# Decode sparse attention inside the input projection: all steps of a tile in one block behind the tile's last product

## The chip, the cores and the metric

The kernel runs on one core of a Trainium2 chip. A core has TensorE (PE in the profile, its weight loads PEld), VectorE (DVE), ScalarE (ACT), GpSimd (POOL) and SyncE (SP), which here only issues transfers. Each engine runs its own list of instructions in order, and they meet through semaphores. Sixteen DMA engines serve the queues of SP, ACT and POOL. The metric is the device time of one launch in microseconds. Differences under 0.5% are what a measurement of this kernel can't tell from none.

## The reference

One inference step of a one-layer decoder with a prompt of 512 rows and 8 sampled sequences of 4 new rows behind 2048 cached positions. Everything is float32.

```python
z = einsum('btd,de->bte', x, w_in) + b_in        # 1024 -> 27 tiles of 128 columns
# mLSTM heads (8): conv of width 4 over q,k; silu; chunkwise recurrence over 64 rows; head norm; sigmoid gate
# sparse attention heads (8 query, 2 key/value), three branches per query, each a masked softmax
s_c = q . k_cmp + bias; o_c = softmax(s_c) . v_cmp      # keys pooled by 32 positions
score = sum of p_c over heads and pairs of pooled blocks # importance of a block of 64
top_i = top_k(score, 16)                                # the current block always in
s_s = q . k[top_i] + bias; o_s = softmax(s_s) . v[top_i]
s_w = q . k_window + bias; o_w = softmax(s_w) . v_window # last 512 positions
mix = concat(mlstm, gate_c*o_c + gate_s*o_s + gate_w*o_w) @ w_out
x1 = LN(ALPHA*x + mix); y = LN(ALPHA*x1 + ffn(x1))      # gated ConvFFN, 2688 wide
```

The keys and values of the 2048 cached positions lie in pages of 128 positions, found through a page table; the last 512 positions have a cache of their own for the window branch.

## The kernel before

Activations are kept transposed, features on the partitions and the 544 rows (512 prompt rows, 32 sampled rows) in the free dimension. A float32 product is made of three fp32r products: ScalarE writes the high part of a weight tile (`split_hi`, L415), VectorE the low part (`split_lo`, L423), two tiles ahead. `project` (L1489) runs the 48 products of one weight tile. SyncE loads weight tiles into a ring of four.

The order of the work is written out by hand, the same on every engine:

1. Input projection, 27 tiles: eight mLSTM q/k tiles (VectorE does the convolution of each, ScalarE the silu), four output-gate tiles, the gate tile `Z_G`, four mLSTM value tiles, four attention query tiles and six attention key/value tiles. Outputs alternate between `q4[0]` and `q4[1]` (banks 0 to 3).
2. Gate transposes and token transposes (L1531, L1555).
3. mLSTM over the prompt (L1559 on) and over the sampled rows (L1634 on).
4. Sparse attention over the prompt (L1690 on). It needs a table of relative biases. It is written to DRAM (`relrow`, L475: the whole of it from 8 partitions) after the last weight load is issued, and read back skewed (`tb`, L479) once it has landed. SyncE waits in between. SyncE also issues there `out_win_s` (4 MB, DRAM to DRAM), `out_zkv`, `out_mconv` and the tiny `out_m_p` (L480 to L486), and waits for them (L488).
5. Sparse attention over the sampled rows, "decode" (L1779 to L1979). Two groups of four sequences. Per group 4 window key bundles (4 transposes each) and 16 quads of pages (`page_keys`: 4 key transposes; `compress`: 8 pooling products). Every fourth quad is followed by a score set (`scores_d`). Bundles of transposes rotate over three banks (`T_BANKS`), and ScalarE copies each to SBUF (`keys_t`, L771). Pages come through a ring of 8 slots in 192 KB transfers (SyncE the even ones, GpSimd the odd ones). Selected values have a place of their own for all 64 pages of a group. Softmaxes, selection (`select`, L1357: a rank by 32 x 32 comparisons in five passes over 1024 elements) and outputs of group g-1 lie between the quads of group g; those of the last group come at the end.
6. Output projection, first norm, 42 up tiles, 24 down parts, second norm.

Where a wait is for a page:

```python
pe.wait_ge(pg_land[o % PAGE_RING], 16 * (o // PAGE_RING + 1))
mm = pe.transpose(t[:, 128 * k:128 * k + 128], pages[:, o % PAGE_RING, 256:384], ident)
```

Of the kernel before, what the change touches and what calls it, by code (L numbers as in the profile page):

```python
# [24 lines left out]
T = 512  # L25
# [18 lines left out]
KEY_BUNDLES = SG + SG * QUADS  # L44
SETS = 1 + QUADS
KEY_RING = 6
T_BANKS = 3
BUNDLES = 1 + KEY_BUNDLES + 2 + 2
LATE = 6
# [14 lines left out]
Z_MQ, Z_MK, Z_MO, Z_G, Z_MV, Z_NQ = 0, 4, 8, 12, 13, 17  # L64
Z_CK, Z_CV, Z_SK, Z_SV, Z_WK, Z_WV = 21, 22, 23, 24, 25, 26
# [3 lines left out]
def table(*widths):  # L69

    at, n = {}, 0
    for name, w in widths:
# [8 lines left out]
                      ("maskw", 512), ("maskn", 64), ("tie", 1024), ("jsum", 128), ("headmask", 8), ("kvmask", 2))  # L81
# [12 lines left out]
def constants():  # L94
# [18 lines left out]
    c["tie"] = np.broadcast_to((r[None, :] < r[:, None]).reshape(1, 1024), (128, 1024))  # L113
# [24 lines left out]
    return a128, a32, rel.astype(f)  # L138


def layer(nc, a):
    with ExitStack() as ctx:
# [26 lines left out]
        tvs = wring[0:32, 3, 0:512]  # L169
        gf = sb("gf", [8, NT])  # L170
# [13 lines left out]
        wpad = sb("wpad", [128, NG * (4 + 80 + CW)])  # L184
# [24 lines left out]
        wslide = wpad[:, 168:].rearrange("p (e c) -> p e c", e=2)  # L209
# [7 lines left out]
        uq = smem[:, 0:1142].rearrange("p (s c) -> p s c", s=2)  # L217
        tq = smem[:, 1142:2284].rearrange("p (s c) -> p s c", s=2)
        hm = smem[:, 2284:2476].rearrange("p (n c) -> p n c", n=8)
        mc = smem[:, 2476:2692].rearrange("p (n c) -> p n c", n=8)  # L220
# [9 lines left out]
        hc = zt[:, 13:17, :].rearrange("p k c -> p (k c)")[:, 0:2048].rearrange("p (j h d) -> p j h d", j=4, h=H)  # L230
# [6 lines left out]
        def by_block(ap):  # L237
# [7 lines left out]
        gd = work[0:32, 3072:3328]  # L245

# [8 lines left out]
        wvs = zt[0:32, 0, 0:512]  # L255
        wks = zt[0:32, 1, 0:512]
# [27 lines left out]
        flat = zt[:, :, :].rearrange("p k c -> p (k c)")  # L284
        pages = wring[:, :, :].rearrange("p s c -> p (s c)")[:, 0:PAGE_RING * 384] \
            .rearrange("p (s c) -> p s c", s=PAGE_RING)

        vsel = [t[:, 0:SG * PAGES * 128].rearrange("p (s k c) -> p s k c", s=SG, k=PAGES) for t in (flat, arena)]
        wk = [w.rearrange("p (k c) -> p k c", k=4) for w in (arena[:, 8192:8704], arena[:, 8704:9216],
                                                            flat[:, 11424:11936], flat[:, 11936:12448])]  # L290
        wvl = arena[:, 9216:11264].rearrange("p (s k c) -> p s k c", s=SG, k=4)
        score = smem[:, :].rearrange("p (g c) -> p g c", g=GROUPS)
        pts = whi_f[:, :, :].rearrange("p s c -> p (s c)")
        biasw = work[:, 0:512]
        biasn = work[:, 512:576].rearrange("p (g c) -> p g c", g=GROUPS)
        biasc = work[:, 576:640]
        skt = [work[:, 640:1152], work[:, 1152:1664], wring[:, 3, 0:512], wring[:, 3, 512:1024],
               zt[:, Z_SV, 0:512], zt[:, Z_WV, 0:512]]
        sw = work[:, 1664:2208]
        pc = work[:, 2208:2272]  # L300
        kct = zt[:, Z_WK, 0:256].rearrange("p (s n) -> p s n", s=SG)
        vcs = work[:, 2400:3424].rearrange("p (b c) -> p b c", b=NB)
        ptw = work[:, 3424:3936]
        ptc = work[:, 3936:4064]
        craw = zt[:, Z_SK, 0:512].rearrange("p (s c) -> p s c", s=SG)
        qb = work[:, 4064:4320].rearrange("p (b m) -> p b m", b=NB)
        rk1 = flat[:, 8704:9728].rearrange("p (j i) -> p j i", j=NBLK)
        rk2 = flat[:, 9728:10752].rearrange("p (j i) -> p j i", j=NBLK)
        gtmp, osb = flat[:, 8704:8752], flat[:, 8704:8832]
        pext = flat[:, 9728:9856]  # L310
        impt, rank, pair = (flat[:, 10752 + 32 * k:10784 + 32 * k] for k in range(3))
        ptn = flat[0:32, 10880:11136].rearrange("p (k c) -> p k c", k=2)
        vnt = flat[0:32, 11136:11392].rearrange("p (k c) -> p k c", k=2)
        st = sm[:, 0:16]
        gr = sm[:, 16:24]
# [53 lines left out]
        v_land = [sem(f"v_land{i}") for i in range(3)]  # L369
        wk_land = sem("wk_land")  # L370
# [7 lines left out]
        nd_ow, nd_o, nd_oc, nd_ot, nd_mx = (sem(n) for n in ("nd_ow", "nd_o", "nd_oc", "nd_ot", "nd_mx"))  # L378
# [51 lines left out]
        def pool_rows(eng, n):  # L430

            page = eng.value_load(ptab[0:1, n:n + 1], min_val=0, max_val=POOL_PAGES - 1)
            return a["pool"][bass.DynSlice(page, 1), :, :].rearrange("a p c -> (a p) c")

        def page_at(o):

            g, u, s, k = o // (SG * PAGES), o // (4 * SG) % QUADS, o // 4 % SG, o % 4
            return (SG * g + s) * PAGES + 4 * u + k

        def page_values(eng, n, rows, landed):  # L440
            g, m = n // (SG * PAGES), n % (SG * PAGES)
            eng.dma_start(vsel[g][:, m // PAGES, m % PAGES, :], rows[:, 384:512]).then_inc(landed, 16)

        def page_keys(eng, o, rows):
            eng.dma_start(pages[:, o % PAGE_RING, :], rows[:, 0:384]).then_inc(pg_land[o % PAGE_RING], 16)

        def stream_page(eng, o, part):

            n = page_at(o)
            if o >= PAGE_RING:  # L450
                rows = pool_rows(eng, n)
                eng.wait_ge(pg_used, o - PAGE_RING + 1)
                page_keys(eng, o, rows)
                if n >= SG * PAGES:
                    page_values(eng, n, rows, v_land[1 + part])
# [4 lines left out]
        def _(sp):  # L460
# [10 lines left out]
            for i in range(2, I_OUT):  # L471
                load_weights(i)
            sp.wait_ge(rel_sb, 1)

            sp.dma_start(relrow.ap(), ohp[0:8, NREL:2 * NREL].unsqueeze(1).broadcast_to([8, 128, NREL])).then_inc(rel_out, 16)  # L475
            sp.wait_ge(rel_out, 16)

            shifted = bass.AP(tensor=relrow, offset=127, ap=[[NREL - 1, 128], [128 * NREL, H], [1, 512]])
            sp.dma_start(tb, shifted).then_inc(tb_in, 16)  # L479
            sp.dma_start(a["out_win_s"], a["win"][:, TS:, :]).then_inc(stored, 16)  # L480
            sp.wait_ge(z_dve, ZT - Z_MV)
            sp.dma_start(a["out_zkv"], zt[:, Z_CK:ZT, :]).then_inc(stored, 16)
            sp.wait_ge(conv_done, Z_MO)
            sp.dma_start(a["out_mconv"], mc).then_inc(stored, 16)
            sp.wait_ge(g_rdy, 1)
            sp.dma_start(a["out_m_p"], lnb[:, T - 1:T]).then_inc(stored, 16)  # L486

            sp.wait_ge(stored, 48 + 16)  # L488
            sp.wait_ge(silu_done, Z_MO)
# [3 lines left out]
            sp.dma_start(n0, a["n0"]).then_inc(sd_in, 16)  # L493
            sp.wait_ge(ml_ce, QT)
# [10 lines left out]

            for n in range(SG * PAGES):
                rows = pool_rows(sp, n)
                page_values(sp, n, rows, v_land[0])
            for o in range(0, PAGE_RING, 2):
                page_keys(sp, o, pool_rows(sp, page_at(o)))  # L510
            sp.wait_ge(np_mx, QT)
            sp.wait_ge(nd_pp, 1)

            def window(b):
                return a["win"][b].rearrange("(k p) c -> p k c", k=4)

            def window_keys(b):
                sp.dma_start(wk[b % SG], window(b)[:, :, 0:128]).then_inc(wk_land, 16)

            def window_values(b):  # L520
                sp.dma_start(wvl[:, b % SG], window(b)[:, :, 128:256]).then_inc(wv_land, 16)

            for s in range(SG):
                window_keys(s)
            for g in range(GROUPS):
                if g >= 1:
                    sp.wait_ge(nd_ow, g)
                for s in range(SG):
                    window_values(SG * g + s)
                for o in range(SG * PAGES * g, SG * PAGES * (g + 1), 2):  # L530
                    stream_page(sp, o, 0)
                    if o == SG * PAGES * g + 4 * SG and g + 1 < GROUPS:

                        sp.wait_ge(nd_s, SETS * g + 1)
                        for s in range(SG):
                            window_keys(SG * (g + 1) + s)
            sp.wait_ge(pg_used, NB * PAGES)
            sp.wait_ge(nd_s, SETS * GROUPS)
            for i in range(I_OUT, I_OUT + RING):
                load_weights(i)  # L540

            sp.wait_ge(nd_mx, GROUPS)
            for k in range(KD):
                sp.dma_start(xt[:, k, :], a["xt"][:, k, :]).then_inc(xin2, 16)
            sp.dma_start(hf, a["hf"]).then_inc(hist, 16)
# [12 lines left out]
        def _(pool):  # L558
# [49 lines left out]
            for o in range(1, PAGE_RING, 2):  # L608
                page_keys(pool, o, pool_rows(pool, page_at(o)))
# [1536 lines left out]
```

## Time and profile before

| | us |
|---|---|
| median of 3 runs | 1099.0 (1095.66 to 1100.27) |
| profiled execution | 1103.59 |
| its span, first to last instruction | 1101.9 |
| TensorE busy | 943.0 (86%) |
| VectorE / ScalarE / GpSimd busy | 535.0 / 359.1 / 78.4 |
| mean granted TensorE clock | 0.859 |

The span divides, by TensorE's instructions, into input projection (12 to 189), token transposes and mLSTM (189 to 306), prompt attention (306 to 424), decode attention (424 to 600), output projection and first norm (600 to 688), up and down projection and second norm (688 to 1102). A granted clock of 1.00 is 2.4 GHz, 0.50 is 1.2 GHz. A busy TensorE is not one at its peak, since matmul records overlap.

### The profile page before, as it was taken

The page shows a single profiled execution, that of the slowest core. Times are in us where ns is not written, and L with a number is a line of the kernel's source. Part 1 is how long each engine was busy: PE and PEld are TensorE (multiplying, and loading weights), DVE is VectorE, ACT ScalarE, POOL GpSimd, SP SyncE. Part 2 cuts the span into 40 slices and gives each one's busy share as a digit, 9 for nine tenths or more (in the row PEclk, how much of TensorE's full clock was granted, in tenths as well). Part 3 has the DMA queues.
Part 4 walks back from the last instruction along what each step waited for, and adds up shares of the span by engine and source line. Part 5 has one row for each costly group of instructions (what it writes and reads, how often), then busy time and mean ns, then how long its engine had stood idle before and what let it go on. Part 6 is the DMA issues. An engine that isn't in the chain of part 4 may idle for free.

```text
span 1101.9 us, 18710 instructions
## 1 busy us (share of the span) xinstructions
PE 943.0 (86%) x7389; PEld 827.2 (75%) x7389; DVE 535.0 (49%) x1095; ACT 359.1 (33%) x729; POOL 78.4 (7%) x124
## 2 busy tenths in 40 slices
PE   4999999875789886677764995999999999999993
PEld 4999999564465554344433984999999999999992
DVE  4653423556546672102526326667666676522225
ACT  3444111211034563113224115443434344322214
POOL 2000100200200000234420000000000000000000
PEclk9999899755556998666576996999999999999997
DMA  7222224361032202778762320222222222222212
GB/s 254 77 97 81 73 79 66 48 274 64 5 115 60 73 1 78 239 210 261 243 215 65 107 77 0 77 87 87 96 78 97 77 96 76 89 85 78 82 48 81
DMA packets 58376, 112.82 MB, mean 102 GB/s; under 512 B 6817, under 2 KB 36290, under 8 KB 57714
## 3 DMA queue, kind: packets, MB, share of 16 engines
q1 hardware_dynamic: 52304, 94.83, 27.2%
q0 software_dynamic: 5120, 14.69, 4.3%
q10 hardware_dynamic: 866, 2.13, 0.5%
q8 instruction: 58, 0.95, 0.3%
q14 instruction: 28, 0.23, 0.1%
HBM read 103.40 MB, written 12.38 MB: 105 GB/s over the span
## 4 chain that ended last, share of the span: by engine, by line
PE 74%; DVE 9%; DMA 7%; ACT 4%; issue 4%; SPq 1%; POOLq 0%; POOL 0%; ACTq 0%; DVEq 0%
PE q L1505 28%; PE q L1503 25%; DMA wring<-in_pool 5%; PE q L1718 2%; PE q L1847 2%; PE q L1746 2%; PE q L1736 2%; PE q L1983 1%; PE q L1606 1%; PE q L1984 1%; DMA xt<-in_xt 1%; PE q L1820 1%; PE q L1660 1%; ACT whi L740 1%; PE q L1708 1%
## 5 line engine op out<-in xcount | busy, mean ns | idle before, releaser
L413 DVE TENSOR_TENSOR wring_r<-wring,whi_r 128x1024 fp32r<-128x1024 f32 (+1 forms) x101 | 121.2, 1201 | 289.6 <-ACT whi_r L410 289.5
L410 ACT ACTIVATE whi_r<-wring 128x1024 fp32r<-128x1024 f32 (+1 forms) x101 | 104.3, 1033 | 390.7 <-PE q L1505 387.3
L1505 PE MATMUL q<-xt_r,whi_r 128*128 128x288 f32 x552 | 165.3, 299 | 0.0
L1503 PE MATMUL q<-xt_r,whi_r 128*128 128x256 f32 x552 | 156.1, 283 | 0.0
L1503 PE MATMUL q<-arena_r,whi_r 128*128 128x256 f32 x440 | 128.2, 291 | 21.6 <-DVE xt_r L413 13.7
L1505 PE MATMUL q<-arena_r,whi_r 128*128 128x288 f32 x440 | 132.1, 300 | 0.0
L1505 PE MATMUL q<-arena_r,wring_r 128*128 128x288 f32 x440 | 131.8, 300 | 0.0
L1503 PE MATMUL q<-arena_r,wring_r 128*128 128x256 f32 x440 | 124.7, 283 | 0.0
L1503 PE MATMUL q<-mixt_r,whi_r 128*128 128x256 f32 x400 | 113.1, 283 | 10.5 <-DVE xt_r L413 10.5
L1505 PE MATMUL q<-mixt_r,whi_r 128*128 128x288 f32 x400 | 119.4, 298 | 0.0
L1503 PEld LDWEIGHTS q<-xt_r,whi_r 128*128 128x128 f32 x552 | 105.4, 191 | 0.0
L1505 PEld LDWEIGHTS q<-xt_r,whi_r 128*128 128x128 f32 x552 | 105.2, 191 | 0.0
L1503 PEld LDWEIGHTS q<-arena_r,whi_r 128*128 128x128 f32 x440 | 84.4, 192 | 23.7 <-DVE wring_r L413 12.7
L1505 PE MATMUL q<-mixt_r,wring_r 128*128 128x288 f32 x336 | 100.1, 298 | 0.0
L1503 PE MATMUL q<-mixt_r,wring_r 128*128 128x256 f32 x336 | 94.4, 281 | 0.0
L1505 PEld LDWEIGHTS q<-arena_r,whi_r 128*128 128x128 f32 x440 | 84.3, 192 | 0.6
L1503 PEld LDWEIGHTS q<-mixt_r,whi_r 128*128 128x128 f32 x400 | 76.1, 190 | 11.1 <-issue 10.9
L1503 PEld LDWEIGHTS q<-arena_r,wring_r 128*128 128x128 f32 x440 | 84.2, 191 | 0.0
L1505 PEld LDWEIGHTS q<-arena_r,wring_r 128*128 128x128 f32 x440 | 84.1, 191 | 0.0
L1505 PEld LDWEIGHTS q<-mixt_r,whi_r 128*128 128x128 f32 x400 | 76.0, 190 | 0.0
L1820 PE MATMUL q<-cst,wring 128*128 128x128 f32 x128 | 40.2, 390 | 27.7 <-DMA wring<-in_pool 27.0
L1503 PEld LDWEIGHTS q<-mixt_r,wring_r 128*128 128x128 f32 x336 | 63.5, 189 | 0.0
(395 smaller groups left out, 1656.3 us busy)
## 6 DMA issues: line engine op xcount, KB each, us to landing
wring<-in_w_up SPq DMA_DIRECT2D x42, 512.0 KB, 3.2
wring<-in_w_in SPq DMA_DIRECT2D x27, 512.0 KB, 3.3
wring<-in_pool POOLq DMA_DIRECT2D x64, 192.0 KB, 3.6
wring<-in_pool SPq DMA_DIRECT2D x64, 192.0 KB, 3.5
wring<-in_w_down SPq DMA_DIRECT2D x24, 448.0 KB, 3.2
zt<-in_pool SPq DMA_DIRECT2D x64, 64.0 KB, 1.9
wring<-in_w_out SPq DMA_DIRECT2D x8, 512.0 KB, 4.2
out_win_s<-in_win SPq DMA_DIRECT2D x1, 4064.0 KB
```

The costliest lines, as they stand in the source:

```text
L410: return eng.activation(out, src, ACT.Copy)
L413: return eng.tensor_tensor(out, src, hi.bitcast(F32), ALU.subtract)
L740: act.activation(ptb[:, m % 2, g, 0:w], bank[4 + g][:, 0:w], ACT.Copy).then_inc(np_te, 1)
L1503: pe.matmul(out[:, 0, 0:HALF], w, x[:, 0:HALF], start=(kk == 0 and n == 0), stop=(end and n == 2))
L1505: mm = pe.matmul(out[:, 1, 0:HALF + NS], w, x[:, HALF:NT], start=(kk == 0 and n == 0), stop=(end and n == 2))
L1606: mm = pe.matmul(bank[4 + q][:, 65 * t:65 * t + 65], whi_f[:, c % 2, 512 * q + 128 * t:512 * q + 128 * t + 128], tv[:, c, 2 * t + q, :], s ...
L1660: mm = pe.matmul(bank[2 + c][0:32, HD * t:HD * t + HD], qm[half(c), t].rearrange("p b x -> p (b x)")[:, 32 * b:32 * b + 32], ctv[half(c), ...
L1718: return pe.matmul(bank[6][p, 128 * j:128 * j + 128], v, probs, start=start, stop=stop, skip_group_check=True)
L1736: mm = pe.matmul(bank[2 * (m % 2) + g][:, 0:w], q_of(GQ * g + j, i), zt[64 * g:64 * g + 64, (Z_SK, Z_WK)[k], 0:w], start=True, stop=True)
L1746: mm = pe.transpose(bank[4 + g][:, 128 * kk:128 * kk + 128], pb[:, m % 3, g, 128 * kk:128 * kk + 128], ident)
L1820: mm = pe.transpose(t[:, 128 * k:128 * k + 128], pages[:, o % PAGE_RING, 256:384], ident)
L1847: mm = pe.matmul(bank[2 + s // 2][32 * k:32 * k + 32, at + 128 * e:at + 128 * e + 128], wslide[:, e, 12 - 4 * u:44 - 4 * u], pg, start=(u ...
```

## The change

The decode attention is no stage of its own. The columns of `w_in` are reordered: gate tile first, then queries (1 to 4), sampled keys and values (5 to 10), the mLSTM q/k tiles (11 to 18), output gates (19 to 22), mLSTM values (23 to 26). The decode work is cut into beats (g, i), i = -4..-1 a window key bundle, i = 0..15 a quad of pages, each of two halves: h = 0 the key transposes, pooling and score set, h = 1 everything else of that beat (softmax steps and outputs, mostly of group g-1). All engines walk the same list of halves. Five halves go to each of tiles 5 to 20, four to each of tiles 21 to 25 and three to tile 26. All halves of a tile run behind its last product.

```diff
+def halves_of_tiles():
+    body = [x for x in decode_halves() if x[0] < GROUPS]
+    tail = [x for x in decode_halves() if x[0] >= GROUPS]
+    out = [[] for _ in range(ZT)]
+    for n, x in enumerate(body):
+        t = len(body) // (TAIL - FIRST)          # FIRST, TAIL = 5, 21
+        out[FIRST + n // t].append((KD - 1, x))
+    for n, x in enumerate(tail):
+        out[TAIL + n // 4].append((KD - 1, x))
 ...
             def project(out, first, parts, hi, lo, kt, split=None, between=()):
 ...
+                        if k == kt - 1:
+                            mm.then_inc(w_used, 1)
+                        for at, half in between:
+                            if at == k:
+                                decode_half(*half)
```

All transposes go through one bank (`bank[5]`), and each bundle waits for the copy of the one before:

```diff
+            def bundle(*name):
+                if BUNDLE[name] >= 1:
+                    pe.wait_ge(nd_te, BUNDLE[name])
+                return bank[5]
 ...
+                    for h in range(NG):
+                        for k in range(4):
+                            pg = pages[:, ring_item(g, i, k) % PAGE_RING, 128 * e + 64 * h:128 * e + 64 * h + 64]
+                            mm = pe.matmul(bank[4][32 * k:32 * k + 32, 128 * s + 64 * e:128 * s + 64 * e + 64],
+                                           wslide[:, e, h, 12 - 4 * u:44 - 4 * u], pg, ...
```

The pooling is thus 16 calls of 64 columns in one bank. The score sets use bank 6 and four key buffers alone. The page ring keeps its 8 slots; window keys go through it too (two slots a bundle), and values through a ring of four slots of 4 x 64 KB. ScalarE and VectorE run a tile's halves ahead of that tile's split and eviction:

```diff
+            for n in range(ZT):
+                for _, half in HALVES[n]:
+                    decode_half(*half)
+                if n + 2 < ZT:
+                    split_hi(act, n + 2)
```

SyncE's list is now (GpSimd's has the other half of the pages and no weights):

```diff
+            for i in range(2, RING):
                 load_weights(i)
+            for n in range(ZT):
+                if n == 4:
+                    sp.wait_ge(rel_sb, 1)
+                    sp.wait_ge(consts, NCONST)
+                    sp.dma_start(relrow.ap(), ohp[0:8, NREL:2 * NREL].unsqueeze(1).broadcast_to([8, 128, NREL])) \
+                        .then_inc(rel_out, 16)
+                    for i in range(-SG, 0):
+                        stream_keys(sp, mybir.EngineType.SP, 0, 0, i)
+                        issued[0] += 1
+                for _, (g, i, h) in HALVES[n]:
+                    stream(sp, mybir.EngineType.SP, 0, issued, g, i, h)
+                if n + RING < I_OUT:
+                    load_weights(n + RING)
```

`stream` asks for the keys of the beats up to two ahead, each slot when it is free, and for a chunk of values when its slot is. The selection is rewritten (`max`, `match_replace` twice, on 32 values) in place of the 32 x 32 comparisons. `tb` is read back behind the whole decode work (`nd_mx`). `out_win_s` and `hf` are issued before the prompt attention ends, the first four output weights at the end of the input projection. The gate exponentials run at tile 4. The results of the decode attention wait in `mixd` and are copied to `mixt` ahead of the prompt attention.

## Rows read from the trace of the kernel before

**Rows 1.** Stages: us, busy us of each engine (instructions), granted clock, DMA share, GB/s
```profile
112.00:191.00 79.00, 78.31 (x609) 77.93 (x609) 26.98 (x49) 10.95 (x11) 4.38 (x3) 0.96 0.29 70
203.00:262.00 59.00, 40.56 (x227) 32.62 (x228) 34.43 (x59) 6.14 (x7) 5.78 (x4) 0.51 0.52 171
424.00:600.00 176.00, 117.56 (x1212) 68.25 (x1212) 46.06 (x95) 44.41 (x98) 49.77 (x93) 0.67 0.63 195
```
**Rows 2.** Timeline, ScalarE's splits released by a tile's end: start, us, what, wait
```profile
60.45 1.06 ACT L410 ACTIVATE whi_r<-wring 128x1024 fp32r<-128x1024 f32 x1 [3.48 <-PE q L1505]
66.49 1.06 ACT L410 ACTIVATE whi_r<-wring 128x1024 fp32r<-128x1024 f32 x1 [3.48 <-PE q L1505]
```
**Rows 3.** Waits, 424 to 600 us: us in total, times, longest
```profile
PE q L1820 <- DMA wring<-in_pool: 27.0, 35, 3.5
```
**Rows 4.** Timeline, first and last instruction of the decode attention
```profile
424.79 1.13 PE L1779 MATMUL q<-cst,relp 128*128 128x512 f32 x2 [0.79 <-DVE mixt L1267]
...
599.12 0.46 DVE L1385 COPY mixt<-q 64x64 f32<-64x64 f32 x2 [0.42 <-PE q L1870]
```
**Rows 5.** Timeline, prices of the decode steps at either clock
```profile
440.43 0.66 PE L1820 MATMUL q<-cst,wring 128*128 128x128 f32 x4
441.01 0.64 PE L1847 MATMUL q<-wring,wpad 128*32 128x128 f32 x16
441.12 0.60 ACT L776 ACTIVATE zt<-q 128x512 f32<-128x512 f32 x1 [2.12 <-PE q L1820]
...
505.12 1.08 PE L1847 MATMUL q<-wring,wpad 128*32 128x128 f32 x16
505.98 1.07 PE L1834 MATMUL q<-wring,xt 128*32 128x512 f32 x2
506.84 1.07 PE L1834 MATMUL q<-zt,xt 128*32 128x512 f32 x2
...
594.09 1.08 PE L1883 MATMUL q<-arena,whi 128*32 128x128 f32 x32
```
**Rows 6.** Page issues: an issue, us to landing by kind, rate of group 1's stretch
```profile
441.24 0.54 POOL L445 DMA_DIRECT2D wring<-in_pool  x1 [0.63 <-issue]
wring<-in_pool POOLq DMA_DIRECT2D x64, 192.0 KB, 3.6
505.00:567.00 62.00, 48.28 (x555) 28.20 (x558) 18.59 (x30) 15.80 (x29) 30.15 (x56) 0.67 0.77 239
```
**Rows 7.** VectorE and ScalarE by form, 424 to 600 us: busy, mean ns, idle before
```profile
L1369 DVE TENSOR_TENSOR smem<-smem,zt 128x2048 f32<-128x2048 f32 x2 | 4.6, 2292 | 0.1
L1316 DVE TENSOR_REDUCE sm<-smem 128x1 f32<-128x2080 f32 x2 | 4.6, 2320 | 0.1
L818 ACT ACTIVATE smem<-smem,sm 128x2080 f32<-128x2080 f32 x2 | 4.1, 2029 | 13.6 <-DVE sm L1317 13.6
```
**Rows 8.** The bias table's transfer: issue, SyncE's wait for it, DMA meanwhile
```profile
164.43 0.88 SPq L475 DMA_DIRECT2D relrow<-smem  x1
SPq L479 <- DMA relrow<-smem: 54.1, 1, 54.1
170.00:180.00 10.00, 10.00 (x82) 10.00 (x81) 4.09 (x6) 2.12 (x2) 0.00 (x0) 1.00 0.43 51
```
**Rows 9.** Small transfers behind large ones of their queue
```profile
5.44 0.34 ACTq L629 DMA_DIRECT2D sm<-in_m  x1
18.21 2.51 POOL L569 COPY mixt<-cst 8x1024 f32<-8x1024 f32 x2 [13.94 <-DMA sm<-in_m]
SPq L490 <- DMA out_m_p<-lnb: 29.2, 1, 29.2
```
**Rows 10.** The clock behind a wait, and in part-busy stretches
```profile
108.00:112.00 4.00, 0.66 (x6) 0.45 (x4) 3.89 (x7) 1.06 (x1) 1.29 (x1) 1.00 0.38 131
112.00:119.00 7.00, 6.31 (x28) 6.31 (x29) 3.36 (x5) 0.00 (x0) 4.22 (x2) 0.51 0.01 2
552.00:557.00 5.00, 3.50 (x65) 2.19 (x63) 0.75 (x1) 1.20 (x2) 3.21 (x6) 1.00 0.94 295
```

More of the change, by code:

```diff
@@ L299, in layer @@
[L299 to L308, printed above, removed]
@@ L444, in page_keys, with page_rows @@
[L444 to L455, printed above, removed]
+        def page_rows(eng, first, step, n):
+            _, ids = nc.values_load_multi_w_load_instructions(ptab[0:1, first:first + step * (n - 1) + 1:step], engines=(eng,),
+                                                              min_val=0, max_val=POOL_PAGES - 1)
+            return [a["pool"][bass.DynSlice(page, 1), :, :].rearrange("a p c -> (a p) c") for page in ids]
@@ L504, in _ @@
             sp.wait_ge(sd_end, 2)
[L506 to L510, printed above, removed]
-            sp.wait_ge(np_mx, QT)
[L512 to L542, printed above, removed]
+            sp.wait_ge(st_cs, 16)
+            sp.wait_ge(stored, 64)
+            sp.dma_start(a["out_win_s"], a["win"][:, TS:, :]).then_inc(stored, 16)
+            sp.dma_start(hf, a["hf"]).then_inc(hist, 16)
+            sp.wait_ge(np_mx, QT)
             for k in range(KD):
                 sp.dma_start(xt[:, k, :], a["xt"][:, k, :]).then_inc(xin2, 16)
-            sp.dma_start(hf, a["hf"]).then_inc(hist, 16)
             for i in range(I_OUT + RING, len(ITEMS)):
@@ L1488, in _, with project @@
         def _(pe):
-            def project(out, first, parts, hi, lo, kt, split=None):
+            def project(out, first, parts, hi, lo, kt, split=None, between=()):
                 for c in range(parts):
@@ new lines, in copied, with on_chip, window_keys @@
+            def copied(*name):
+                pe.wait_ge(nd_te, BUNDLE[name] + 1)
+            def on_chip(g, i, k):
+                o = ring_item(g, i, k)
+                pe.wait_ge(pg_land[o % PAGE_RING], 16 * (o // PAGE_RING + 1))
+                return pages[:, o % PAGE_RING, :]
+            def window_keys(g, i):
+                t = bundle("keys", g, i)
+                for w in range(2):
+                    chunk = on_chip(g, i, w)
+                    for k in range(2):
+                        mm = pe.transpose(t[:, 256 * w + 128 * k:256 * w + 128 * k + 128], chunk[:, 128 * k:128 * k + 128],
+                                          ident)
+                mm.then_inc(nd_t, 1)
@@ new lines, in scores_d @@
+            def scores_d(g, j):
+                n = SETS * g + j
+                copied("keys", g, SG * j - 1)
+                if n >= 1:
+                    before, was = (n - 1) // SETS, (n - 1) % SETS
+                    if was == 0:
+                        pe.wait_ge(nd_wr, before + 1)
+                    else:
+                        pe.wait_ge(nd_se, QUADS * before + was)
+                for s in range(SG):
+                    mm = pe.matmul(bank[6][ROWS * s:ROWS * s + ROWS, :], qb[:, SG * g + s, :], skt[s], start=True, stop=True)
+                mm.then_inc(nd_s, 1)
@@ new lines, in window_t, with output @@
+            def window_t(g, new):
+                pe.wait_ge(nw_p, g + 1)
+                t = bundle("window", g, new)
+                if new:
+                    mm = pe.transpose(t[0:32, 0:128], sw[:, 512:544], ident)
+                else:
+                    for k in range(4):
+                        mm = pe.transpose(t[:, 128 * k:128 * k + 128], sw[:, 128 * k:128 * k + 128], ident)
+                mm.then_inc(nd_t, 1)
+            def output(s, probs, v, start=False, stop=False):
+                return pe.matmul(bank[7][ROWS * s:ROWS * s + ROWS, 0:128], probs[:, ROWS * s:ROWS * s + ROWS], v,
+                                 start=start, stop=stop, skip_group_check=True)
@@ new lines, in outputs_window @@
+            def outputs_window(p):
+                copied("window", p, True)
+                copied("new_values")
+                pe.wait_ge(wv_land, 16 * SG * (p + 1))
+                if p >= 1:
+                    pe.wait_ge(nd_mx, p)
+                for s in range(SG):
+                    output(s, ptn[:, 1, :], vnt[:, 1, :], start=True)
+                for k in range(4):
+                    for s in range(SG):
+                        mm = output(s, ptw[:, 128 * k:128 * k + 128], vring[:, k, s, :])
+                    mm.then_inc(v_used, 1)
@@ new lines, in importance_t, with outputs_compressed @@
+            def importance_t(p):
+                pe.wait_ge(nc_pr, p + 1)
+                t = bundle("importance", p)
+                pe.matmul(t[:, 0:32], k128("jsum"), pair, start=True, stop=True)
+                pe.wait_ge(nc_p, NG * (p + 1))
+                pe.transpose(t[:, 128:256], pext, ident).then_inc(nd_t, 1)
+            def outputs_compressed(p):
+                copied("importance", p)
+                for s in range(SG):
+                    output(s, ptc, vcs[:, s, :].unsqueeze(1).broadcast_to([128, NG, HD]))
@@ new lines, in selected_t @@
+            def selected_t(p, k):
+                pe.wait_ge(ns_p, 5 * p + k + 1)
+                t = bundle("selected", p, k)
+                if k < 4:
+                    for c in range(4):
+                        mm = pe.transpose(t[:, 128 * c:128 * c + 128], score[:, p, 512 * k + 128 * c:512 * k + 128 * c + 128],
+                                          ident)
+                else:
+                    mm = pe.transpose(t[0:32, 0:128], score[:, p, PAST:SCW], ident)
+                mm.then_inc(nd_t, 1)
```

1174 lines of the change are left out of this document (618 added, 556 removed).

## The prediction

> **What bounds the kernel now.** I read the table of stages first, then the waits of the stage that moves, then single instructions for prices. The input projection is dense: TensorE is busy 79 of 79 us at nearly full clock, a tile every 6.04 us [rows 1, 2]. The decode attention is the opposite: 176 us in which TensorE is busy 118 at a mean clock of 0.67 while DMA moves 195 GB/s [rows 1]. Its largest wait on TensorE is for pages, 27.0 us [rows 3]. From its first product at 424.79 to its last copy at 599.58 [rows 4] nothing of the other stages runs: 174.8 us on the path, and all of it goes. The question is what the same work costs behind 22 of the 27 tiles (5 to 26), since TensorE does it between two tiles and not beside them.
>
> **The change part by part.** Sums are for the profiled execution, 1103.6 us with a span of 1101.9; the median of the three timed runs, 1099.0, is 4.6 lower, and I subtract the same 4.6 at the end.
>
> *TensorE's own decode work.* At full clock four key transposes take 0.58 us (440.43 to 441.01), a quad's pooling (8 calls, 16 records) about 0.57, 16 output calls 1.08 (32 records at 594.09) [rows 5]. Per group of four sequences: 20 key bundles x 0.58 = 11.6; 16 poolings. These become 16 calls of 64 columns instead of 8 of 128: not below 0.57 (same columns), not above 1.08 (what the old form takes at half clock, when each call costs double); I take 0.65, near the low end, because the columns that pass are the same and four calls run beside each other on 32 array columns each: 10.4. Five score sets: four calls of 512 columns are 8 records in two waves 0.85 apart at half clock (505.98, 506.84, the last ending at 507.91) [rows 5]; I take 1.0 at full: 5.0. 92 output calls, 16 in 1.08 with the last one's tail: 5.8. 28 other transposes x 0.145: 4.1. Small products: 1. That is 38, twice 76 us.
>
> *Waits in the blocks.* (a) All bundles now share one bank (bank 5), so each waits for ScalarE's copy of the one before: 0.60 us [rows 5] and two hand-overs, 0.85. Behind a page bundle the pooling covers 0.65: 32 x 0.2 = 6. Behind the eight window bundles nothing does: 6. Behind some 20 others 5. Together 17. (b) Pages. The ring holds 2 beats (8 pages). Five halves a tile are 3 page beats in tiles 7, 9, 11, 15, 17, 19 and 2 in the others. Two beats lie ready when a block begins, since 6 us of projection cover them; the third is asked for when the first is used up. Two issues per queue at 0.54 and 3.6 to landing [rows 6] make 4.7, less one beat (1.43) in between: 3.2 x 6 = 19. SyncE's weight loads queue behind these page requests, but four weights are in the ring, so they are not late. (c) Values: four chunk slots, asked for two beats before use in the same block. With 4 issues x 0.54 and 3.6 to landing, 5.8 less some 1.7 of work: 4 each in tiles 24 and 25, 2 in tile 18: 10. (d) Chains. Tile 23 waits for select and softmax: the bias and the maximum over 2048 scores are 2.29 and 2.32, the exp 2.03 [rows 7], plus the new selection (six small DVE operations, at about 0.2 as the others of 32 to 64 columns) and a table load. That makes 9.8, of which 6.0 are covered by tile 23's products. The old ranking (five passes over 1024 elements) is gone from this chain. Tiles 13 and 21 run scores, ScalarE's compressed copies, transposes and scores again in one block, 2 each. Together 8. Sum of waits 54; blocks 76 + 54 = 130 us, or 5.9 us per tile. VectorE and ScalarE take 46 and 44 us of decode work into a phase that is now about 300 us long; their own loads there, 27 and 11 in 79 us of its second half [rows 1], leave room, and splits are a tile ahead.
>
> *A transfer that is moved.* The bias table's rows (relrow, 2560 KB from 8 partitions) went out at 164.43, after the last weight load; SyncE then stood 54.1 us until they had landed, and nobody noticed, as nothing was due [rows 8]. Meanwhile DMA stood at a share of 0.43 and 51 GB/s: a slow transfer that fills some 7 of 16 engines. In the new order it is issued after tile 3 (about 43 us: 42.3 and 0.9 of set-up), with tile 5's window keys right behind it on the same queue. Is a queue served in order? ScalarE's last constant, 1 KB, was issued at 5.44 and freed GpSimd at 18.21; out_m_p, a few bytes behind the 4 MB of out_win_s, kept SyncE for 29.2 us [rows 9]. So small transfers do wait behind large ones of their queue. Window keys of SyncE's half then land at 43 + 55 + 1 = 99 us. Tile 5 ends at about 59: before, tile 6 ended at 60.4 [rows 2], tile 5 at 54.4; 1.2 come on for the gate transposes that stood behind the last tile and 3.6 for set-up (below). TensorE waits 40 us in the first block, with all queued behind it. From both sides: 0, if rows of one queue overtake each other, or 45, if GpSimd's half of the keys shares those engines. I take 40, the value of the two rows.
>
> *Clock.* One wait of 4.0 us in the old projection (for a tile's eviction, 108 to 112) was followed by 7 us at 0.51, i.e. at 1.2 GHz, then 2.4 GHz again [rows 10]: half of 6.8 us is lost, 3.4. I count the blocks with a wait of 3 us or more: 5, 7, 9, 11, 15, 17, 19, 23, 24, 25, ten x 3.4 = 34. Bounds: 0, if busy ends of a block keep the clock, and 22 x 3.4 = 75.
>
> A rule of the Trainium skill speaks against the change here. "TensorE: Matmul & The Clock Gate", section "HAM oscillation — how this bites in real kernels": short bursts of products separated by waits for DMA start every burst at the half rate. By it each of the 21 later blocks costs its 3.4, a sum 37 us higher than mine; the decode stage of before (0.67) goes with the rule, the wait of 4.0 us shows one such fall.
>
> *Small terms.* Set-up products now ahead of tiles 2 and 5 add 0.9 + 0.6, and tile 5 waits 2.1 for the sample queries (copies of 0.74, 0.24 and small ones): 3.6. The gate tile comes first, so the 4.0 us wait and its clock loss go: -7.4. Exponentials of the gates are ready long before the mLSTM (ScalarE's table load 1.28 after the token transposes stood on its path): -2.5. Output weights and history, read earlier, are hidden before and after. The 4 MB window copy moves under the prompt attention (51 GB/s there, share 0.17 over 118 us, so room): 0; if that cover failed its 29 us would have to be met by the reload of xt.
>
> Sum: 130 + 40 + 34 + 3.6 - 7.4 - 2.5 = 198, against 174.8: +23 us, 1127 in the profiled execution, **1122 us** against the median.
>
> **Rivals.** (1) *The table's rows do not hold up the queue.* Then the 40 us go and its clock fall: 1122 - 43 = 1079, faster. It decides by the moment SyncE's first window keys land: before 76 us (99 - 23) the change gains. For it: nothing in the trace ran behind relrow, and a share of 0.43 leaves over half of the engines free; against it: the two waits of [rows 9]. (2) *Full clock and covered waits.* Blocks end in products, and page beats keep TensorE some 85% busy; clock 0 to 7 instead of 34, which gives 1088 to 1095, faster. For it: 552 to 557 ran at 1.00 with TensorE 70% busy [rows 10]. Against: a wait of 3 us stands in six blocks. (3) *The clock falls at every block*, since even a block without a page wait leaves TensorE idle during each copy: 22 falls of 3.4 instead of 10, 1122 + 41 = 1163. For it: 203 to 262, TensorE busy 41 of 59 us in gaps of 1 to 4 us, had 0.51 [rows 1]. Against: after the one wait of 4.0 the clock was back within 7 us, and blocks of 4 us hold 3 of products. It is the case of the skill's rule above. (4) *DMA becomes the bound* in group 1: 12.6 MB keys, 5.3 values, 1.1 window keys, 4.2 weights, 1.7 output, 24.8 MB, at 239 GB/s [rows 6] 104 us for tiles 13 to 20, where my blocks and products come to 8 x 6.04 + 53 + 10 = 112. So it costs nothing unless the rate falls below 221; at 200 it adds 12.
>
> **How the numbers follow.** Forecast with its mechanism (with or without (4)) 0.54, its own range 1100 to 1145; (1) 0.16; (2) 0.16; (3) 0.14. A measurement of this kernel tells 0.5%, 5.5 us, from no change. Of the forecast's 0.54, 0.06 lies within 0.5% (waits and clock at their low ends); of (1) 0.13 is faster and 0.03 the same; of (2) 0.15 and 0.01. So faster 0.28, same 0.10, slower 0.62. The range reaches from (1) into (3): 1075 to 1168.
>
> **What would show it.** After: TensorE idle from about 59 to 99 us, with SyncE's window keys as releaser (right), or tile 6's products at about 63 (rival 1). Block lengths alternating by 3 us between tiles 7 and 12; a granted clock of 0.5 in the first microseconds of the products behind tiles 7, 9, 11, 1.00 behind 8 and 10 (rival 3: behind all). End of the projection at about 188 + 200 = 388 us; the prompt attention followed within 1 us by the output projection. My forecast is wrong if the blocks cost over 7 or under 5 us a tile beside the first, or if ScalarE's order (a wait for VectorE's maximum ahead of a key copy) stops TensorE for long, which I have put at nothing because each such step falls behind a page wait.

## The result and the profile after

| | before | after |
|---|---|---|
| timed runs, median (range) | 1099.63 us (1095.66 to 1101.08) | 1109.92 us (1106.5 to 1112.78) |
| profiled execution; its span | 1103.59; 1101.9 us | 1106.5; 1104.4 us |
| mean granted clock | 0.859 | 0.879 |

The kernel is slower: the ratio is 1.0112, with an interval of 1.0083 to 1.0141, so 9 to 15.5 us. The two profiled executions lie only 2.9 us apart: the one of after was the fastest of its four, the one of before (1103.59) was slower than all four timed ones. I had subtracted the same 4.6 us on both sides; what follows accounts for the profiled 2.5 us of span, and the other 8 us between the medians can't be read from a trace.

The stages of after, by windows (columns as in [rows 1]): the last products of tile 5, the wait behind them, and everything from there to the last product of the projection.

```profile
53.00:61.50 8.50, 8.47 (x48) 8.35 (x48) 0.00 (x0) 0.00 (x0) 0.00 (x0) 0.70 0.43 49
61.50:101.70 40.20, 3.06 (x13) 2.19 (x13) 0.00 (x0) 1.19 (x2) 1.12 (x2) 0.54 0.49 79
101.70:369.30 267.60, 225.54 (x2716) 192.93 (x2714) 87.90 (x172) 93.73 (x176) 78.35 (x136) 0.91 0.57 179
```

One window holds three key bundles and nothing else for 40 us. Then 21 tiles (6 to 26) with 20 blocks between them (a block is the decode work behind a tile's last product) run with TensorE 84% busy at a clock of 0.91, against 67% and 0.67 in the old decode stage [rows 1]. TensorE's waits between 50 and 370 us (total, times, longest), which answer to [rows 3]:

```profile
PE q L1653 <- DMA arena<-in_win: 35.8, 1, 35.8
PE q L1733 <- DMA arena<-in_pool: 15.3, 8, 3.6
PE q L1661 <- DMA arena<-in_pool: 8.9, 10, 1.5
PE q L1767 <- DVE smem L1188: 5.5, 1, 5.5
```

These are the window keys, the values, the pages and the selected probabilities. SyncE's own timeline shows why the first is long: its four requests for window keys took 37.2 us to issue behind the table's rows, where the same four take 2.9 us elsewhere (below).

```profile
41.50 0.86 SPq L568 DMA_DIRECT2D relrow<-smem  x1
42.40 37.20 SPq L505 DMA_DIRECT2D arena<-in_win  x4
79.64 10.89 SPq L555 DMA_DIRECT2D wring<-in_w_in  x1
```

Now the blocks. Windows over the products of tile 7, the block behind them (three page beats), the products of tile 8 and those of tile 9:

```profile
113.16:119.16 6.00, 6.00 (x54) 6.00 (x48) 2.64 (x4) 1.07 (x2) 1.07 (x2) 1.00 0.65 221
119.28:126.10 6.82, 4.02 (x110) 2.75 (x108) 0.00 (x0) 1.67 (x3) 2.15 (x4) 1.00 0.54 178
126.10:133.62 7.52, 7.52 (x54) 7.52 (x48) 2.04 (x3) 1.07 (x2) 1.08 (x2) 0.77 0.64 226
138.43:144.43 6.00, 6.00 (x53) 6.00 (x48) 3.12 (x7) 1.07 (x2) 1.07 (x2) 1.00 0.86 291
```

A tile is 6.00 us of products at full clock; tile 8 took 7.52 because part of it ran at 1.2 GHz (0.77 in the mean), tile 9 was whole again. Inside the block of tile 7 the third beat waits for its pages (timeline; the bracket is the idle time and what ended it):

```profile
121.16 0.65 PE L1673 MATMUL q<-arena,wpad 128*32 128x64 f32 x32
123.31 0.30 PE L1661 MATMUL q<-cst,arena 128*128 128x128 f32 x1 [1.49 <-DMA arena<-in_pool]
124.46 0.44 PE L1661 MATMUL q<-cst,arena 128*128 128x128 f32 x2 [0.85 <-DMA arena<-in_pool]
125.26 0.33 PE L1661 MATMUL q<-cst,arena 128*128 128x128 f32 x1 [0.36 <-DMA arena<-in_pool]
```

From last product to first product (the last 0.3 us of the last product counted in) the blocks of tiles 6 to 12 took 3.59, 6.94, 4.81, 6.46, 4.00, 8.14 and 2.59 us. The longest are 19 (12.58), 24 and 25 (11.22 and 11.25): values are what they wait for. The projection ends at 369.0 us, and the output projection begins at 604.62.

### The profile page after: what moved, and what is told of

Its sections match the earlier page's. It is cut to its first block, busy times and chain, and to the rows that moved or that the text cites. A ratio compares the mean times of both kernels' runs of the same rounds, so it can differ in the third digit from the quotient of the medians.

```text
span 1104.4 us, 19843 instructions
## 1 busy us (share of the span) xinstructions
PE 925.0 (84%) x7903; PEld 826.8 (75%) x7903; DVE 520.7 (47%) x1100; ACT 373.2 (34%) x742; POOL 99.5 (9%) x164
## 4 chain that ended last, share of the span: by engine, by line
PE 72%; DVE 8%; issue 5%; ACT 5%; another core or an unknown queue 3%; DMA 3%; SPq 3%; POOLq 1%; POOL 0%; ACTq 0%; DVEq 0%
PE q L1624 28%; PE q L1622 25%; DMA arena<-in_pool 3%; PE q L2061 2%; PE q L2079 2%; PE q L2089 2%; PE q L1949 1%; PE q L2003 1%; PE q L2122 1%; PE q L2123 1%; SPq L477 1%; PE q L1661 1%; PE q L1673 1%; DVE xt L1486 1%
## 5 line engine op out<-in xcount | busy, mean ns | idle before, releaser
L1624 PE MATMUL q<-xt_r,whi_r 128*128 128x288 f32 x552 | 168.4, 305 | 0.0
L1622 PE MATMUL q<-xt_r,whi_r 128*128 128x256 f32 x552 | 158.9, 288 | 0.0
L1622 PE MATMUL q<-arena_r,whi_r 128*128 128x256 f32 x440 | 133.4, 303 | 19.9 <-DVE xt_r L458 11.8
L1624 PE MATMUL q<-arena_r,whi_r 128*128 128x288 f32 x440 | 135.1, 307 | 0.0
L1624 PE MATMUL q<-arena_r,wring_r 128*128 128x288 f32 x440 | 134.4, 305 | 0.0
L1622 PE MATMUL q<-arena_r,wring_r 128*128 128x256 f32 x440 | 127.3, 289 | 0.0
L1622 PE MATMUL q<-mixt_r,whi_r 128*128 128x256 f32 x400 | 112.9, 282 | 10.6 <-DVE xt_r L458 10.5
L1622 PEld LDWEIGHTS q<-xt_r,whi_r 128*128 128x128 f32 x552 | 108.5, 197 | 0.0
L1624 PEld LDWEIGHTS q<-xt_r,whi_r 128*128 128x128 f32 x552 | 108.3, 196 | 0.0
L1622 PEld LDWEIGHTS q<-arena_r,whi_r 128*128 128x128 f32 x440 | 87.8, 199 | 22.6 <-DVE wring_r L458 11.7
L1624 PEld LDWEIGHTS q<-arena_r,whi_r 128*128 128x128 f32 x440 | 87.5, 199 | 0.6
L1622 PEld LDWEIGHTS q<-arena_r,wring_r 128*128 128x128 f32 x440 | 87.1, 198 | 0.0
L1624 PEld LDWEIGHTS q<-arena_r,wring_r 128*128 128x128 f32 x440 | 86.9, 197 | 0.0
L744 ACT ACTIVATE mixt<-q 128x512 f32<-128x512 f32 x40 | 23.9, 596 | 144.1 <-PE q L1661 82.6
```

The source lines that it names most:

```text
L744: act.activation(skt[i % SG], t, ACT.Copy).then_inc(nd_te, 1)
L1622: pe.matmul(out[:, 0, 0:HALF], w, x[:, 0:HALF], start=(kk == 0 and n == 0), stop=(end and n == 2))
L1624: mm = pe.matmul(out[:, 1, 0:HALF + NS], w, x[:, HALF:NT], start=(kk == 0 and n == 0), stop=(end and n == 2))
```

## The experiments

Times are ratios to the kernel before, run on the same chip in turn; "against after" is their quotient with 1.0112 times 1099. Edits are against the changed kernel where nothing else is said.

**Table rows on ScalarE's queue.**

```
-  sp.dma_start(relrow.ap(), ohp[0:8, NREL:2 * NREL] ...)      # SyncE, n == 4
+  act.dma_start(relrow.ap(), ohp[0:8, NREL:2 * NREL] ...)     # ScalarE, n == 4
```

> The changed kernel, with one move: the bias table's rows (2560 KB from 8 partitions) go out on ScalarE's DMA queue instead of SyncE's, at the same point (after tile 3). Queue theory (window keys stood behind these rows on one queue): the wait of 35.8 us in the first block goes and that block falls from 40.4 to about 5 us, so the time is 33 to 38 us below the changed kernel's 1109.9, about 1074; SyncE's four window-key issues no longer take 37 us. Rival (the rows keep 8 of the 16 DMA engines busy, and any transfer beside them is slow, whatever its queue): window keys still land after 80 us, the first block keeps over 20 us, and the time stays above 1095.

Measured: 1.0005 (0.9978 to 1.0031), 12 us below after. Neither theory holds alone. The queue is a third of it: SyncE's requests no longer stand 37 us, and the first keys are there sooner. But they come one by one, behind waits of 4.5, 6.0 and 6.0 us. SyncE's issues, then TensorE's waits in the first block (timelines):

```profile
42.06 15.78 SPq L505 DMA_DIRECT2D arena<-in_win  x4
```
```profile
66.48 1.11 PE L1654 MATMUL q<-cst,arena 128*128 128x128 f32 x4 [4.51 <-DMA arena<-in_win]
73.64 1.09 PE L1654 MATMUL q<-cst,arena 128*128 128x128 f32 x4 [6.04 <-DMA arena<-in_win]
80.73 1.09 PE L1654 MATMUL q<-cst,arena 128*128 128x128 f32 x4 [6.01 <-DMA arena<-in_win]
```

The blocks of tiles 5, 6, 7 took 19.8, 10.5 and 8.2 us here (40.4, 3.6, 6.9 in after). In the trace's packets the rows are 1024 packets of 2560 bytes, 0.36 us each in the steady stretch and some 19 a microsecond: seven engines' worth. The keys are packets of 512 bytes, 0.03 us each. In after, half of each key request (128 of 256 packets) passed at 62 to 81 us while the rows went out, and the other halves came together at 94 to 98. That the first halves went by the engines left free and the second by those that the rows filled is my reading: the records name no engine. With a queue of their own the keys' packets pass between the long ones, some 19 a microsecond like these. So the larger part is the share of the engines, and a second queue only lets the small transfers take turns. The Trainium skill says this of two issuing engines ("DMA: Bandwidth & Descriptors", section "Issuing engines are not separate DMA queues": all run on the same 16 engines and interleave); by it the second queue saves only the time to issue. This run agrees in that some 25 us of the 37 stayed. What it saved is 12 us, and SyncE's four issues fell from 37.2 to 15.8.

**Table rows behind the window keys.** The two statements at n == 4 on SyncE are swapped.

> The changed kernel, with one swap on SyncE's queue: the four window-key requests first, the bias table's rows behind them. Theory (the rows hold up whatever is behind them on the queue and what shares their DMA engines): the first block falls to about 5 us, but the next page requests are behind the rows, so the block of tile 6 takes over a wait that ends near 100 us; the time is 0 to 8 us below the changed kernel's 1109.9. Rival (it was only the place ahead of the first keys that hurt): over 25 us gained.

Measured: 1.0042 (1.0017 to 1.0067), 8 us below after: as the theory had it, at the end of its range. The block of tile 5 took 3.17 us, that of tile 6 took 33.5:

```profile
41.12 2.93 SPq L505 DMA_DIRECT2D arena<-in_win  x4
44.10 0.87 SPq L571 DMA_DIRECT2D relrow<-smem  x1
48.38 16.93 SPq L555 DMA_DIRECT2D wring<-in_w_in  x1
70.27 5.01 SPq L513 DMA_DIRECT2D arena<-in_pool  x2
```
```profile
101.35 1.08 PE L1661 MATMUL q<-cst,arena 128*128 128x128 f32 x4 [28.97 <-DMA arena<-in_pool]
```

**One part of the change alone, in the kernel before.** The rows go out between weights 7 and 8.

```
     for i in range(2, I_OUT):
+        if i == 8:
+            sp.wait_ge(rel_sb, 1); sp.wait_ge(consts, NCONST)
+            sp.dma_start(relrow.ap(), ohp[0:8, NREL:2 * NREL] ...)
         load_weights(i)
```

> The kernel before, with one move: the bias table's rows go out on SyncE's queue between weights 7 and 8 of the input projection (about 42 us) instead of behind the last weight. Queue theory: weight 8 lands only once the rows are out, near 100 us; TensorE stands from the end of tile 7 (about 66) to about 102, and the kernel takes 33 to 40 us more, about 1136. Rival (rows overtake each other on a queue, or the stall of the changed kernel had another cause): weight 8 lands within some microseconds and the time stays within 5 us of before.

Measured: 1.0342 (1.0309 to 1.0376), 37.5 us slower. TensorE stood at the place named, with a weight as the late piece (its low part, which VectorE makes, is what ends the wait), and there is no decode work near it. This run does not tell the queue from the engines either, since a weight could be held up by both:

```profile
101.38 0.55 PE L1505 MATMUL q<-arena_r,whi_r 128*128 128x256 f32 x1 [35.05 <-DVE wring_r L413]
```

**One row per head.** The table is stored as it is (20 KB); the 128 copies are made from DRAM behind the last tile.

```
+  relone = nc.dram_tensor("relone", (H, NREL), F32, kind="Internal")
-  sp.dma_start(relrow.ap(), ohp[0:8, NREL:2 * NREL].unsqueeze(1).broadcast_to([8, 128, NREL])) ...
+  sp.dma_start(relone.ap(), ohp[0:8, NREL:2 * NREL]) ...                  # n == 4
+  sp.dma_start(relrow.ap(), relone.ap().unsqueeze(1).broadcast_to([8, 128, NREL])) ...  # behind ZT
```

The bias (`tb`) is loaded behind the output weights here.

> The changed kernel, with the table stored after tile 3 as one row per head (20 KB instead of 2560 KB); the 128 copies are made from that row, DRAM to DRAM, behind the last tile of the projection, and the bias is loaded behind the output weights. Nothing slow is left beside the first blocks. Theory (the 40 us are the rows' transfer: its place on the queue and the engines that it fills, and the run with the rows on ScalarE's queue kept most of the second): the first block takes about 6 us, blocks 6 to 8 fall back to 4 to 7, and the time is 32 to 38 us below the changed kernel, 1072 to 1078. Rival (the stall gives way to another one of like size, page requests that bunch up or the clock): above 1090. If the bias comes late, a wait for it stands in the prompt attention.

Measured: 0.979 (0.9767 to 0.9813), 35 us below after and 23 below before. SyncE's four key requests take 2.7 us, and TensorE's three bundles follow with 0.69 us for a copy between them:

```profile
41.31 0.35 SPq L569 DMA_DIRECT2D relone<-smem  x1
41.71 2.73 SPq L506 DMA_DIRECT2D arena<-in_win  x4
```
```profile
60.49 0.60 PE L1655 MATMUL q<-cst,arena 128*128 128x128 f32 x4
61.78 0.66 PE L1655 MATMUL q<-cst,arena 128*128 128x128 f32 x4 [0.69 <-ACT mixt L746]
63.12 0.66 PE L1655 MATMUL q<-cst,arena 128*128 128x128 f32 x4 [0.69 <-ACT mixt L746]
```

The block takes 3.29 us, so 37.1 of its 40.4 were the rows' transfer. At the projection's end 35 of them are left (334 against 369 us): the stretch behind the first block, by a window like that of after, is 270.5 us long and not 267.6.

```profile
63.50:334.00 270.50, 223.60 (x2717) 189.90 (x2715) 87.89 (x172) 93.79 (x176) 78.68 (x136) 0.91 0.60 188
```
```profile
318.48 0.83 SPq L585 DMA_DIRECT2D relrow<-relone  x1
```

The new copy has a place of its own to answer for. SyncE issues it at 318.48, behind its own last requests, while GpSimd's last values are still on their way and TensorE waits for them in the block of tile 25; that block takes 14.8 us here and 11.25 in after. The last of its waits for values, in which the copy runs, is 3.43 us here and 0.26 in after. No run moved the copy alone, so that it costs these 3 us is likely and not shown.

**Control.** The same in the kernel before, at the old place.

> Control: the kernel before with the bias table stored as one row per head and copied 128 times DRAM to DRAM, at its old place behind the last weight. Theory (the 54 us of the rows' transfer cost only where something is due behind or beside them): nothing waits there, the time stays within 3 us of before, though SyncE stands for far less than 54 us. Rival (the slow transfer also cost the kernel before something): more than 5 us faster, and a part of the gain of the kernels with one row has nothing to do with the order.

Measured: 1.001 (0.9981 to 1.004), as the theory had it: the slow transfer costs only where something is due.

**Halves spread over a tile's products.**

```
-        out[FIRST + n // t].append((KD - 1, x))
+        out[FIRST + n // t].append(((0, 2, 4, 5, 7)[n % t], x))
-        out[TAIL + n // 4].append((KD - 1, x))
+        out[TAIL + n // 4].append((2 * (n % 4) + 1, x))
```

> The changed kernel, with the same halves in the same order and in the same tiles, but behind products k = 0, 2, 4, 5, 7 of a tile (1, 3, 5, 7 in tiles 21 to 26) instead of all behind k = 7. Theory (in the blocks TensorE waits some 42 us for copies, pages, values and chains, tiles 6 to 25, which products could cover, and 16 us go to half clock): the wait of 40 us for the window keys stays, the other 267.6 us up to the end of the projection shrink by 30 to 50, time 1060 to 1080. Bound that may stop it: keys, values and weights of tiles 5 to 26 are about 50 MB, at 239 GB/s 210 us. Rival (the order of ScalarE and VectorE, which do a tile's decode copies ahead of its splits and evictions, makes tiles wait instead): less than 10 us gained, with TensorE waiting at the start of tiles for weight splits or evictions.

Measured: 0.9834 (0.9803 to 0.9865), 31 us below after; the median of 1081 is just above the theory's 1060 to 1080, and the stretch shrank by 22 us, not by 30 to 50. The stall of 40 us is still there; from 98 us on (window):

```profile
98.20:343.70 245.50, 222.62 (x2766) 191.52 (x2764) 88.32 (x174) 94.94 (x178) 79.28 (x137) 0.96 0.63 198
```

TensorE is busy for 223 us again, but the window is 22 us shorter and the clock is 0.96 in place of 0.91: TensorE's idle time in it fell from 42 to 23 us. The waits for pages fell from 8.9 to 3.2 us, for values from 15.3 to 10.6; the 5.3 us for the last selection stayed. The rival's waits at a tile's start did not come.

**Both.**

> The one row per head and the halves spread over a tile's products together. Theory (two separate losses): their gains add, 35 + 27 below 1109.9, that is 1044 to 1052, the projection ends near 308 us. Rival (with both gone DMA is the bound: keys, values and weights of tiles 13 to 20 are 25 MB): the gains add to less than 52, above 1058, TensorE waits for pages in tiles 13 to 20 and the DMA share there is over 0.8.

Measured: 0.9505 (0.948 to 0.9529), 67 us below after; 35 and 31 add. DMA is not the bound in the densest stretch:

```profile
140.00:226.00 86.00, 77.01 (x1082) 63.56 (x1085) 41.35 (x82) 45.56 (x88) 32.57 (x61) 0.98 0.75 237
```

**Both, with the last selection given a tile to itself.** Counts 6, 3, 2, 4, 4, 4 in place of 4, 4, 4, 4, 4, 3.

> As the kernel with both, and the last group's 23 halves lie 6, 3, 2, 4, 4, 4 over tiles 21 to 26 instead of 4, 4, 4, 4, 4, 3, so that the last selection (ranking, mask, maximum, exponential) has all of tile 23 beside it. Theory (TensorE waited 5.3 us for the scaled probabilities): that wait goes, 3 to 6 us faster than the kernel with both. Rival (the values' waits grow by as much): within 1.5 us of it.

Measured: 0.9453 (0.9431 to 0.9475), 1038.1 us, 5 to 6 us below the one before it. The wait for the probabilities (5.3 us) is gone; part comes back as waits for values (14.9 us in all, 12.1 in the run before). In the tail GpSimd needs 4.3 us for the four values of a chunk, and the chunks come at that pace. The longest of the waits, a third of the sum, stands at the end, with the copy of the table's rows under way since 283.98:

```profile
270.67 2.31 POOL L530 DMA_DIRECT2D arena<-in_pool  x4 [1.97 <-issue]
274.95 2.31 POOL L530 DMA_DIRECT2D arena<-in_pool  x4 [1.97 <-PE q L1737]
```
```profile
291.49 0.66 PE L1737 MATMUL q<-arena,cst 128*32 128x128 f32 x8 [5.11 <-DMA arena<-in_pool]
```

**The new selection alone, in the kernel before.** The five passes give way to the changed kernel's max, match_replace, max, memset, match_replace and compare.

> The kernel before, with the selection of the changed kernel alone (two maxima of eight and two replacements over 32 columns instead of five passes over 32 x 32). Theory: the ranking of the last group of sequences lies on the path behind the last page, so its five passes of about 1 us each fall to below 2 us together: 3 to 6 us faster, the first group's stays hidden. Rival: the chain is covered by the window and compressed outputs, and the time stays within 1 us.

Measured: 0.9961 (0.9937 to 0.9984), 4 us faster. From the first pass to the mask's addition the ranking takes 1.37 us (1.22 us a pass and 6.4 in all before); VectorE's timeline:

```profile
575.03 0.19 DVE L1361 MAX8 zt<-zt 128x8 f32<-128x32 f32 x1 [0.80 <-ACT zt L814]
...
575.98 0.17 DVE L1365 MATCH_REPLACE8 zt<-zt 128x32 f32<-128x32 f32 x1
576.18 0.18 DVE L1366 TENSOR_SCALAR zt<-zt 128x32 f32<-128x32 f32 x1
576.40 2.29 DVE L1369 TENSOR_TENSOR smem<-smem,zt 128x2048 f32<-128x2048 f32 x1
```

## Why the prediction was right, and where it was not

The sign was right, the stall that decides it stood where I had put it, and the time of 1109.9 lies in the forecast's own range; the forecast of 1122 was 12 too high. Two terms came out for reasons that were in part not mine: the stall's cause, and the sum of the blocks. By its steps, in the profiled executions:

- **The stall, 40 us: right in place and size, in its cause by a third.** 40.4 us in the first block, of which the block's own work is 3.3 (one row per head), so 37.1. The move of the rows alone in the kernel before costs 37.5. The two rows of [rows 9] carried it, against the rival that the rows do not block (1079). My "small transfers do wait behind large ones of their queue" is too narrow, though: the run with a second queue kept two thirds of the loss. I had written of engines that the transfer fills, and gave them only the 5 us between 40 and the upper bound of 45, for GpSimd's half of the keys (that half was asked for at 16.36 and stood behind nothing); they are the larger part. Both readings put the stall at the same place, so the number could not tell them apart.
- **Blocks, 130 us: right in the sum, with some luck.** Tiles 6 to 25 took 127.9, with 3.3 for block 5's own work 131. The prices nearly held: a pooling is 0.65 as taken, TensorE is busy 80 us in the 20 gaps, where I had 76 for all 22 blocks; and each length above holds 0.3 us of the last product, 6 in all, which I had not counted. Its idle time in these gaps is 42 us and not 54, and that makes up for it. The waits inside were shared out wrongly: pages 8.9 us, not 19, and values 15.3, not 10, the chain of tile 23 5.5, not 4 (the terms that I named for it add to 9.1, not 9.8, with the table load at 1.28). A page wait of a block is up to 2.7 us in three pieces (block 7) where I had 3.2; and I had counted values in tiles 18, 24 and 25, but it is block 19 that waits for them (2.7 us), and not 18. Lengths alternate as forecast between tiles 7 and 12.
- **Clock, 34 us: the step that was mis-sized.** It measured 15.6, as the excess over 6.00 us of tiles 5 to 26. The number of falls was nearly right: I named ten blocks, and nine were followed by a slowed tile (5, 7, 11, 15, 16, 19, 23, 24, 25), eight of them mine; 16 was not on my list, 9 and 17 were and had none. The size was not: I took 3.4 us each from the one fall of [rows 10], and the nine lost 0.95 to 1.98, tile 5 another 2.25 behind its wait for the sample queries. Part of the low clock lay inside the long blocks, where there is less to lose:

```profile
268.80:281.26 12.46, 8.03 (x156) 5.01 (x154) 0.18 (x1) 2.96 (x6) 6.13 (x12) 0.81 0.81 244
281.26:288.22 6.96, 6.96 (x51) 6.96 (x48) 1.89 (x2) 4.82 (x7) 3.51 (x7) 0.85 0.71 199
331.47:342.69 11.22, 4.75 (x76) 2.91 (x74) 0.00 (x0) 0.60 (x1) 5.32 (x10) 0.79 0.42 110
342.69:349.64 6.95, 6.95 (x49) 6.95 (x48) 2.04 (x3) 1.54 (x2) 3.24 (x7) 0.84 0.46 128
```

  These are windows over blocks 19 and 24 of after and the tile behind each: the block already ran at 0.81 and 0.79, and the tile lost one microsecond more. A block of 6.27 us (16) was followed by a fall and one of 7.28 (18) was not; what decides it these traces do not show. The rival of a fall at every block (1163) fell. I had called it the case of the Trainium skill's rule ("TensorE: Matmul & The Clock Gate", section "HAM oscillation — how this bites in real kernels"), by which every burst behind a wait for DMA starts at the half rate. The page's case is a wait longer than the burst before it, with nothing in between. The blocks here hold products in between (TensorE was busy 4.8 of 11.0 us in that of tile 25, and all of the 1.6 in that of tile 22), so I had stretched the rule; a slowed tile stands behind nine blocks of 21.
- **End of the projection 388: was 369.0.** Blocks and stall together 168.3 for 170, clock 15.6 for 34, the small terms of this stretch -3.1 for -3.8; the clock is the difference.
- **Between the projection's end and the output projection: 4.1 us gained, where I had 2.5 for the exponentials** (235.6 us for the 239.7 that are left of before without its decode stage; before begins the output projection at 602.75); 0.6 us lost behind that. So 180.8 us longer to the end of the projection, 174.8 for the removed stage, -4.1 and +0.6: +2.5 us of span, where the forecast had 23. The clock is 18 of the 20 us between them.
- **The other rivals.** Full clock and covered waits (1088 to 1095): fell, by the nine falls and by 30 us of waits for pages, values and probabilities; it was nearer than I thought. DMA as the bound: fell, also in the faster kernel with both edits, at a share of 0.75 and 237 GB/s in the stretch shown, above the 221 from which it would have decided.

So the change lost by one transfer. With the table as one row per head the whole change is worth 23 us, and the stall cost 35. That is shown: the run takes away the slow transfer, and the same edit in the kernel before changes nothing (1.001). What of the 23 us belongs to the place of the decode work alone is not told apart from the changes that came with it; the new selection by itself gave 4 us in the old order.

## What to carry to other kernels

When a stage moves, list every DMA that moves with it and its engine share: a transfer nobody waited for, at 51 GB/s and a share of 0.43 [rows 8], became the critical path as soon as something small was due beside it, and another queue was only a third of a remedy; make it small, or leave it where nothing is due. Insert short dependent work between single products of the dense stage rather than in a block behind it: more of the same copies and page loads was then covered, and the clock stood higher, here for 31 us. And price clock losses from more than one fall.

## What the hardware showed that I had not expected

- The same 128 copies (1024 packets of 2560 bytes) take 54 us read from eight SBUF partitions and 15 us read from DRAM, at a DMA share that is much the same. SyncE's timeline of the control, and windows over the copy, whole and in its steady stretch:

```profile
166.24 0.80 SPq L478 DMA_DIRECT2D relrow<-relone  x1
181.48 0.40 SPq L482 DMA_DIRECT2D arena<-relrow  x1
```
```profile
166.00:181.00 15.00, 15.00 (x122) 15.00 (x121) 4.17 (x8) 2.12 (x2) 0.00 (x0) 1.00 0.45 176
170.00:180.00 10.00, 10.00 (x82) 10.00 (x81) 4.09 (x6) 1.06 (x1) 0.00 (x0) 1.00 0.52 208
```

A packet took 0.10 us in place of 0.36. In ten steady microseconds the share is 0.52, with 208 GB/s, where [rows 8] has 0.43 and 51: about half of the 16 engines from either source. So the outer size of eight, which both have, and not the source, goes with the half; what makes the packets from SBUF slow no run here tells. The Trainium skill has the rule for the count ("DMA: Bandwidth & Descriptors", section "Why a DMA increments its semaphore by 16 and not by 1": the largest number up to 16 that divides the outer sizes on both sides, here 8). That is a share of 0.50, and the two shares lie on either side of it; an outer size of 16 was not tried.

- A request's packets overtake: half of each 128 KB key request was through at 62 to 81 us, before the large transfer ahead of it on its queue had ended (97 us), yet its completion came only with the other half, at 94 to 98.
